# High parts behind the exponentials, modulation in the norm chains, and low parts shared by two engines

## The reference, cut to what matters

```python
h = rms_norm(x, norm_mix_pre[l])
proj = h @ w_in[l]                       # q, kv, gates of branch a, d, conformer, pooling
k_cmp = nsa_compress(k, ...)             # blocks of 32 keys -> 15 keys by a small MLP
o_a = g0 * o_cmp + g1 * o_slc + g2 * o_win   # three attentions over 8 heads
o_b = silu(layer_norm(causal_depthwise_conv(a * sigmoid(gate))))   # 31 taps
o_c = pool_mixer(c_in, pool_w[l], pool_scale[l])
o_d = banded_attention(..., SWA_WINDOW, swa_sinks[l])
up = einsum("bsnc,ncd->bsnd", [o_a, o_b, o_c, o_d], w_branch[l])
gates = sigmoid(h @ w_gate[l])           # 1024 x 4096
mix = sum_n(gates * up) @ w_o[l]
x = x + rms_norm(mix, norm_mix_post[l])
u = causal_depthwise_conv(rms_norm(x, ...) @ ffn_w_up[l], ffn_conv_w[l], ...)
x = x + rms_norm((gelu(gate) * val) @ ffn_w_down[l], norm_ffn_post[l])
```

## Time and profile before

| | |
|---|---|
| median of three runs | 2239.13 us |
| profiled execution, its span | 2239.11 us, 2237.3 us |
| TensorE matmul busy | 1869.7 us (84%) |
| VectorE, ScalarE, GpSimd busy | 1047.0, 754.9, 382.2 us |
| mean granted clock of TensorE | 0.879 |
| high parts in the first block (L404) | 118 of 1912 ns, ScalarE idle before them 404.2 us, of which 251.8 for a DMA |
| low parts by GpSimd (L410) | 26 of 4610 ns, 119.9 us |
| weight chunks | 256 of 1 MB, 4.8 us from issue to landing |

### The profile page before, as it was taken

The page is one execution under the profiler, slowest core; times in us unless marked ns, Lnnn a source line. Parts: engine busy times, 40 slices in busy tenths (PEclk is TensorE's granted clock), DMA queues, the critical chain, the costliest instruction groups (busy, mean ns, idle before and its releaser), DMA issues. The chain is left out here.

```text
span 2237.3 us, 26793 instructions
## 1 busy us (share of the span) xinstructions
PE 1869.7 (84%) x10780; PEld 1507.6 (67%) x10780; DVE 1047.0 (47%) x1452; ACT 754.9 (34%) x1055; POOL 382.2 (17%) x311
## 2 busy tenths in 40 slices
PE   7876767887988787676788799899989998899996
PEld 5765545877986566554587798654447653789996
DVE  4472324456653447232445665312844432545555
ACT  4332233444542333223344454211222330333341
POOL 0122220122540012222012244010142000100000
PEclk9987778898999898777889899979987999789998
DMA  5533122343545352313234354532211004235452
GB/s 216 201 110 132 76 113 94 114 151 123 188 159 198 108 206 106 132 76 112 94 115 150 125 186 166 191 138 72 79 38 38 1 1 150 76 133 188 179 179 92
DMA packets 39390, 279.99 MB, mean 125 GB/s; under 512 B 4464, under 2 KB 4720, under 8 KB 6384
## 3 DMA queue, kind: packets, MB, share of 16 engines
q1 hardware_dynamic: 37984, 272.44, 33.5%
q10 hardware_dynamic: 1296, 6.00, 0.7%
HBM read 277.37 MB, written 1.05 MB: 124 GB/s over the span
## 5 line engine op out<-in xcount | busy, mean ns | idle before, releaser
L404 ACT ACTIVATE sb_hi<-ring 128x2048 fp32r<-128x2048 f32 x118 | 225.7, 1912 | 404.2 <-DMA ring<-weights 251.8
L410 DVE TENSOR_TENSOR ring_low<-ring,sb_hi 128x2048 fp32r<-128x2048 f32 x92 | 211.7, 2303 | 231.6 <-ACT sb_hi L404 231.6
L545 PE MATMUL psum<-sb_hS,sb_hi 128*128 128x256 f32 x704 | 225.0, 320 | 40.3 <-DVE ring_low L410 25.2
L548 PE MATMUL psum<-sb_hS,sb_hi 128*128 128x256 f32 x704 | 218.6, 310 | 0.0
L549 PE MATMUL psum<-sb_hS,ring_low 128*128 128x256 f32 x704 | 216.9, 308 | 0.0
L777 PE MATMUL psum<-sb_hfT,ring_low 128*128 128x256 f32 x704 | 198.0, 281 | 0.0
L545 PEld LDWEIGHTS psum<-sb_hS,sb_hi 128*128 128x128 f32 x704 | 155.8, 221 | 55.5 <-DVE ring_low L410 32.1
L410 POOL TENSOR_TENSOR ring_low<-ring,sb_hi 128x2048 fp32r<-128x2048 f32 x26 | 119.9, 4610 | 426.0 <-ACT sb_hi L404 426.0
L1701 DVE TENSOR_TENSOR sb_split<-ring,sb_split 128x2048 fp32r<-128x2048 f32 x48 | 110.0, 2292 | 160.1 <-ACT sb_split L1696 160.1
L548 PEld LDWEIGHTS psum<-sb_hS,sb_hi 128*128 128x128 f32 x704 | 155.6, 221 | 0.0
L549 PEld LDWEIGHTS psum<-sb_hS,ring_low 128*128 128x128 f32 x704 | 155.5, 221 | 0.0
(11 more groups left out here) (382 smaller groups left out, 4392.1 us busy)
## 6 DMA issues: line engine op xcount, KB each, us to landing
ring<-weights SPq DMA_DIRECT2D x256, 1024.0 KB, 4.8
sb_rows<-rows ACTq DMA_DIRECT2D x1, 2048.0 KB, 9.8
sb_cols<-cols ACTq DMA_DIRECT2D x2, 694.0 KB, 6.2
sb_rows<-rows ACTq DMA_DIRECT2D x2, 516.0 KB, 6.9
sb_x<-x_in SPq DMA_DIRECT2D x1, 1024.0 KB, 5.1
sb_rows<-rows ACTq DMA_DIRECT2D x2, 512.0 KB, 3.7
sb_y<-ctx_in SPq DMA_DIRECT2D x1, 1024.0 KB, 5.6
out<-sb_x SPq DMA_DIRECT2D x2, 512.0 KB, 2.6
```

Of the source, the lines that this page charges most:

```text
L404: act.activation(hi_of(n), ring[:, c % SLOTS, :], ACT.Copy).then_inc(hi_ready, 1)
L410: eng.tensor_tensor(low_of(n), ring[:, SPLIT_CHUNKS[n] % SLOTS, :], hi_of(n).bitcast(F32), ALU.subtract)\
L545: mm = pe.matmul(out, hi[:, k, bs], hS[:, 0, k, :], start=(k == 0), stop=False)
L548: pe.matmul(out, hi[:, k, bs], hS[:, 1, k, :], start=False, stop=False)
```

## The change

It rearranges the first block's layers; the second block's program is not changed.

- **Attention.** In ScalarE's order the high part (`gate_hi`) stands behind the probability copies and the exponentials of the item. The modulation chunks are gone from this stretch. One padding chunk lies among the gates (behind the eighth) to keep the count at 92.
- **Low parts of gates 0 to 13** are made in two halves, columns 0 to 1023 by GpSimd and 1024 to 2047 by VectorE; TensorE waits for both.
- **Before attention.** The chunks of the compression MLP and those of ba and bg alternate (raw, ba, raw, ba, raw, bg, raw, bg). Pooling matmuls, compressed keys and compressed scores move behind gate 0 and gate 1, with their work on ScalarE and VectorE.
- **Modulation.** Three steps (six chunks) come after the output projection, three after the down projection of each layer. The rows are turned before and behind the transposes of the norm; the additions on VectorE follow in the norm chain.
- **FFN start.** The high and low parts of its first chunks are made later in the chain, the first low part ahead of the scaling of the turned rows.
- **Down projection** in the regions s0, s1, t and u.

```diff
-    out = ["split"] * 12 + ["raw"] * 4 + ["split"] * 2
-    for i in range(16):
-        out.append("split")
-        if mid_mod_of(i) is not None:
-            out.append("raw")
-    return out + ["split"] * (12 + FFN_CHUNKS) + ["raw"]
+    mods = ["raw"] * MOD_STEPS
+    gates = ["split"] * PAD_GATE + ["raw"] + ["split"] * (16 - PAD_GATE)
+    return ["split"] * FIRST_BA + ["raw", "split"] * 4 + gates + ["split"] * 12 + mods + ["split"] * FFN_CHUNKS + mods
...
+    for name in (("hid", 0), ("ba", 0), ("ba", 1), ("hid", 1), ("bg", 0)):
+        jobs.plan(name)
+    jobs.plan(("hidT", 0), "t", drains=2)
...
+    for i, r in zip(MODS_WO, "tus"):
+        jobs.plan(("mod", i), r)
+        jobs.plan(("modT", i), r)
...
-            jobs.plan(("down", c, t), f"a{2 * t + c}", drains=2)
+            jobs.plan(("down", c, t), ("s0", "s1", "t", "u")[2 * t + c], drains=2)
+    for kind in ("mod", "modT"):
+        for i in MODS_DOWN:
+            jobs.plan((kind, i))
...
     def split_lo(eng, n):
-        assert (n in POOL_LOWS) == (eng is nc.gpsimd)
+        half = slice(0, CH) if n not in POOL_LOWS else slice(CH // 2, CH) if eng is nc.vector else slice(0, CH // 2)
         eng.wait_ge(hi_ready, n + 1)
+        eng.tensor_tensor(low_of(n)[:, half], ring[:, SPLIT_CHUNKS[n] % SLOTS, half], hi_of(n)[:, half].bitcast(F32), ALU.subtract)\
+           .then_inc(lo_dve if eng is nc.vector else lo_pool, 1)
...  TensorE, attention
                 gate_chunks(1)
+                if i == 0:
+                    pool_mix()
+                    cmp_keys()
                 if i == 1:
+                    cmp_scores()
+                    gate_chunks(1)
                     cmp_out()
...  TensorE, behind the output projection
+            for i in MODS_WO:
+                mod_half(i, 0)
+                mod_half(i, 1)
+            for i in MODS_WO[:-1]:
+                mod_turn(i)
             for c in range(2):
                 for t in range(TT):
                     transpose4(("hf", c, t), ...)
+            mod_turn(MODS_WO[-1])
...  TensorE, behind the down projection
+            for i in MODS_DOWN:
+                mod_half(i, 0)
+                mod_half(i, 1)
+            for i in MODS_DOWN:
+                mod_turn(i)
...  ScalarE, attention
+            exps(0)
+            gate_out(1)
+            pool_out()
+            gate_hi()
+            for i in range(1, len(ITEMS) + 1):
                 if i >= 2:
                     out_copy(i - 2)
+                gate_out(1)
                 if i == 1:
+                    gate_hi()
+                    cmp_exps()
                     gate_out(1)
                     for t in range(TT):
                         copy_out(("cpT", t), ...)
+                turned_out(i - 1)
                 if i < len(ITEMS):
                     exps(i)
+                gate_hi()
...  VectorE, attention
+            mask(0)
+            split_lo(dve, FIRST_GATE + 1)
+            conv_steps(12)
+            pool_low()
+            cmp_blocks()
+            split_lo(dve, FIRST_GATE + 2)
+            for i in range(1, len(ITEMS) + 1):
                 if i < len(ITEMS):
                     mask(i)
+                weigh(i - 1)
...
                 conv_steps(10)
+                if i == 1:
+                    cmp_mask()
+                    cmp_weigh()
+                if FIRST_GATE + i + 3 in POOL_LOWS:
+                    split_lo(dve, FIRST_GATE + i + 3)
...  VectorE, norm chain behind the output projection
             residual("wo", 2)
-            split_lo(dve, FIRST_FFN + 1)
             dve.wait_ge(squares, 2 * TT)
             norm_tiles(3)
-            split_lo(dve, FIRST_FFN + 2)
+            mods_in(MODS_WO[:-1])
+            split_lo(dve, FIRST_FFN)
```

More of the change, by code:

```diff
@@ L261, in plan_layer @@
             jobs.plan(("O", a, t), "u", drains=2)
-    for i in range(16):
+    for i in range(2, 16):
         jobs.plan(("gate", i))
[L264 to L268, removed]
     for t in range(TT):
@@ L562, in _, with hid_half, hid_turn @@
                 transpose4(("rkT", t), [rot[:, t, i * P:(i + 1) * P] for i in range(3)])
[L563 to L580, removed]
+            def hid_half(kv, half):
+                chunk = next_chunk().rearrange("p (l h) -> p l h", l=8)
+                if half == 0:
+                    jobs.claim(pe, ("hid", kv))
+                    pe.wait_ge(flat_ready, 4 * kv + 5)
+                for lp in range(8):
+                    mm = pe.matmul(jobs.out(("hid", kv))[32 * (lp % 4):32 * (lp % 4) + 32, 0:T], flat32[:, kv, 8 * half + lp, :],
+                                   chunk[:, lp, :], start=(half == 0 and lp < 4), stop=(half == 1 and lp >= 4))
+                    if lp == 0:
+                        carry(mm)
+                if half == 1:
+                    jobs.fill(mm, ("hid", kv))
                 release(("hid", kv))
-            release(blocks_fm(("bg", 0)))
-            for kv in range(2):
+            def hid_turn(kv):
                 jobs.wait_drained(pe, ("hid", kv))
@@ L591, in _ @@
                 jobs.fill(mm, ("hidT", kv))
[L592 to L612, removed]
+            for kv in range(2):
+                for half in range(2):
+                    hid_half(kv, half)
+                    if (kv, half) == (1, 1):
+                        hid_turn(0)
+                        jobs.wait_drained(pe, "ga")
+                        jobs.claim(pe, "gaT")
+                        for t in range(TT):
+                            mm = pe.matmul(jobs.out("gaT")[:, 24 * t:24 * t + 24], gaT[:, t * P:(t + 1) * P], K("sel", 0, 24), start=True, stop=True)
+                        jobs.fill(mm, "gaT")
+                    release(blocks_fm((("ba", "bg")[kv], half)))
+            hid_turn(1)
             for t in range(TT):
@@ L617, in _ @@
                 transpose4(("rdT", t), [rot[:, t, 896 + i * P:896 + (i + 1) * P] for i in range(4)])
[L618 to L624, removed]
@@ L1320, in _ @@
                                   ALU.subtract).then_inc(mix_lo, 1)
-            for n in range(FIRST_WO + 1, FIRST_FFN + 1):
+            for n in range(FIRST_WO + 1, FIRST_FFN):
                 split_lo(dve, n)
@@ L2807, in rows_split @@
     return w.reshape(-1, 2, P, D).transpose(0, 2, 1, 3).reshape(-1, P, CH)
-def gates_and_mods(gate, mod):
-    out = []
-    for n in range(16):
-        at = 4 * BRANCH_ORDER[n // 4] + n % 4
-        out.append(gate[at:at + 1])
-        step = mid_mod_of(n)
-        if step is not None:
-            out.append(mod[step][n % 2:n % 2 + 1])
-    return out
 def layer_inputs(l, i):
@@ L2828, in layer_inputs @@
     br = {0: pairs(br[0], DH, 0), 1: br[1], 2: br[2], 3: pairs(br[3], DH, 0)}
+    cmp = i["nsa_cmp_w1"][l].reshape(2, 2, 8, P, 256).transpose(0, 1, 3, 2, 4).reshape(4, P, CH)
+    gate = n_split(i["w_gate"][l])
+    gate = [gate[4 * n + b] for n in BRANCH_ORDER for b in range(4)]
     chunks = [
```

265 lines of the change are left out of this document (143 added, 122 removed).

## The result

| | before | after |
|---|---|---|
| median of four runs each | 2239.67 us | 1984.27 us (1982.47 to 1987.12) |
| ratio, 95% interval | | 0.8861 (0.8846 to 0.8877) |
| profiled execution, its span | 2239.11, 2237.3 | 1983.36, 1981.6 |
| TensorE matmul busy (10780 matmuls in both) | 1869.7 | 1793.0 |
| span less that busy time | 367.6 | 188.6 |

The time fell by 255.4 us. Forecast was 2000.0 (1972 to 2070). The spans differ by 255.7: 179.0 is idle time of TensorE that went, and 76.7 is shorter matmuls. Their number is the same, so I read the second share as clock.

What follows compares the result with a forecast made beforehand. Attention was taken as bound by a chain: gate matmuls' end, transfer, high part, probability copy, value matmuls. Per layer -21 -52 -50 -7 +4 +6 = -120, two layers -240, from 2239 to 1999, rounded 2000 us (1972 to 2070).

Steps and rivals of the forecast that it cites:

- Part 1: Attention items: landing wait goes, small items 9.7 us, large 12.3; -52 and -50 us per layer.
- the two chains: Large items: TensorE's own work, 11.8 us, against a chain over all engines ending in VectorE's weighting, 11.8 or 12.4.
- Part 2: Low parts in halves: the engines exclude one another, VectorE first, 3.4 us; 0.65 per small item (absorbed), nothing in large.
- Part 3: Before the items: first ba block 7.7 us later, repaid by transfers no longer piling up; -21 us per layer.
- Part 4: Up to down projection: the 6.79 us idle before the down matmuls goes; -7 us per layer.
- The term of low clock: Down projection: about 1 us of low clock behind the stall there also goes.
- Part 5: Modulation in the norm chains: matmuls free, transfers not; FFN start +4, after the down projection +6 us per layer.
- The fourth rival: Faster: no slip in items (11.8 and 9.5), chains only +2 and +4; about 1985 us, within the forecast's own range.
- The first (the chain stays): Attention copies bound by something other than landing, only TensorE's moved modulation work goes; 2207 us, chance 0.06.
- The second (GpSimd first): GpSimd takes the lock first, each low part keeps VectorE 2.3 us longer; 2054 us, chance 0.18.
- the third: Slower: norm-chain modulation transfers one by one at 6.1 us, items still bound as before; 2333 us, chance 0.03.

Runs made afterwards that it cites:

- Run 3: The changed kernel with the low parts of gates 0 to 13 made whole on VectorE, none on GpSimd; 1996.92 us.
- run 4: The changed kernel with the low parts of gates 0 to 13 made whole on GpSimd, none on VectorE; 1999.31 us.
- run 6: The changed kernel with ScalarE's second ba high part behind the c and q copies, VectorE's low part behind its two copies, compressed mask and weights before the taps; 1955.96 us.
- Run 5: The changed kernel with the down projection back in the old banks a0 to a3; 2004.11 us.
- run 1: The changed kernel with ScalarE's high part put back ahead of the probability copies and exponentials in every attention item; 2063.02 us.

## Why the prediction came out, step by step

Times are of the first layer.

- **Part 1, items.** Small: 9.2 to 10.0 us from values to values (predicted 9.7). Large: 11.5 to 12.3 (12.3). Two sums of the prediction are not what their terms give: 1.16, 5.8, 0.66, 0.7 and 1.0 add to 9.3, not 9.5, and the terms of the large item to 11.7, not 11.8. The 2.3 us for a first item at the low clock did not come either: it took 9.5 us. From the third item to the first large one 48.1 us (51.6), from there to the end of the gates 81.3 (84): together -108 per layer in place of -102. The granted clock stayed at 1.00, for which the prediction had one pair of rows. In a large item VectorE's weighting ends at 240.84 and the transposes start at 240.89, so the two chains do tie; in the next two items TensorE waits 0.60 and 0.71 us for the weighting. Run 3 shows that a longer VectorE chain costs at once.
- **Part 2, halves.** The taps ahead of the third item, then VectorE and GpSimd in a small item:

```profile
145.27 6.20 DVE L1184 SCALAR_TENSOR_TENSOR sb_acc<-sb_bglu,sb_cols,sb_acc 128x256 f32<-128x256 f32 x10
...
161.28 1.22 DVE L395 TENSOR_TENSOR ring_low<-ring,sb_hi 128x1024 fp32r<-128x1024 f32 x1 [6.07 <-ACT sb_hi L388]
...
163.95 0.85 DVE L1259 TENSOR_TENSOR sb_small<-sb_small 128x4 f32<-128x4 f32 x1
164.83 0.69 DVE L1262 TENSOR_TENSOR sb_sc<-sb_sc,sb_small 128x512 f32<-128x512 f32 x1
```

```profile
161.39 3.39 POOL L395 TENSOR_TENSOR ring_low<-ring,sb_hi 128x1024 fp32r<-128x1024 f32 x1 [13.76 <-ACT sb_hi L388]
```

  VectorE goes first, as forecast, in 25 of the 28 low parts of the two layers. GpSimd's 3.39 us hold 1.11 of waiting (until 162.50) and 2.28 of work, the estimate being 2.26. The small product then waits until GpSimd is done at 164.78, 0.69 us longer than its 0.16; 0.65 was priced. Mask and maximum run beside GpSimd. The Trainium skill ("SBUF — State Buffer", section "Who interferes with whom") has this as a lock that the first to issue holds for its whole instruction; this trace and run 4 agree (2.67 us for a 128x4 product). Not priced was the place ahead of the third item: the ten taps at 145.27 stand behind the low part with GpSimd's half (144.24, 3.38 us) waiting, and took 6.20 us in place of 4.04. The compressed weights follow them, so by these rows some 2.2 of the 5.14 us wait for those weights come from the shared low part; no run tests that.
- **Part 3.** Transposes at 89.86 (predicted: with the copy at 90.5), first ba block 92.5 (92.8), first scores 124.4 (127.4), second item 134.0 (138.8), the wait for the compressed weights 5.14 us (about 5), third item 160.8 (163.5). Against before that is -24 instead of -21. The prediction read the new stall off the ring (which slot a chunk falls into), and run 6 shows that only an order of two instructions stood behind it: it could have been avoided. No run undoes the new order ahead of attention, so its -24 is read from the two traces alone.
- **Part 4.** The down projection follows the FFN without a gap and takes 61.5 us, 63.3 before: -8.6 where -7 was taken. Run 5 prices it at 20 us for both layers. The term of low clock was too small: without the stall the projection runs 1.8 us faster in the first layer here, and 2.8 in run 5.
- **Part 5.** FFN starts at +25.7 (predicted 24.7), +5 instead of +4. The next layer's transposes come at 29.7 behind the down projection, 19.4 before: +10.3 instead of +6. By its share this is the term that was mis-sized most. The last halves took 1.93 us and each turn 1.76, as TensorE was at the low clock, where the prediction had 1.07 and about 1.0; the last modulation sum came 18.9 us after the end, not 15.7. The end of layer 2, which has less behind it, moved by 6.2.
- **Sum.** Layer 1: -24 -56 -52 -8.6 +5 +10.3 = -125, and TensorE's first projection of layer 2 starts at 620.93 instead of 745.84. Layer 2 and the step into the second block bring 130: -24.1, -108.4 and -8.0 for the same places, and +4.9 and +6.2 for the chains. Predicted were 120 each. The 15 us between: parts 1, 3 and 4 brought 6 + 3 + 1.6 more per layer, 21 in all, and part 5 took 5.3 more in layer 1 and 1.2 in layer 2. So the forecast is near partly by luck, as these misses have opposite signs. The fourth rival (1985) is the nearest by its number, and that is luck too: its small items (9.5) and large ones (11.8) are about what came, but its chains (+2 and +4) cost +5 and +10.3, and it needed the larger gains of parts 3 and 4 to come out.
- **Rivals.** The first (the chain stays) fell by the trace. The second (GpSimd first) fell as well: it needs VectorE's low parts at 3.4 us, and they are at 1.22 in the items. Once per layer, behind the second item's scores (at 135.92 in the first), GpSimd did start first, and VectorE's low part took 2.08. Of the third, chunks came 6.1, then about 2.5 apart, as forecast.

## What to carry to other kernels

When an instruction waits for a DMA, look at what stands behind it in its engine's order before touching the transfers: moving a few lines gave 178 of 255 us by itself (79 on top of the rest of the change), and the late transfer stayed late. A queue in program order should have its waits sorted by who needs the result first, at the start of a stage too (run 6, 28 us more). Price a stall in a matmul stage twice, as idle time and as clock behind it: in run 1 the two were equal, in run 5 the clock was about a third of the idle time. Prefetched work put into idle chains is free only up to the depth of the ring.

## What the runs showed of the hardware

- One stall of 2.5 us in each item of 11 to 19 us brought the granted clock to 0.82 on average in the large items (run 1). Some items behind such a stall ran at the full clock and others at 1.2 GHz, where the scores took 3.78 us. A stall of 0.7 us, or two in a large item, left it at 1.00 in the changed kernel. The Trainium skill ("TensorE: Matmul & The Clock Gate", section "HAM oscillation — how this bites in real kernels") describes a loop of short bursts and waits for a DMA in which every wait takes the clock down. Run 1 agrees that waits which recur cost clock, with busy time up by 37.5 us at the same number of matmuls, but not that each one does, and its waits are shorter (2.5 us, against 3 to 5 in the page's loop) and are for a ScalarE copy.
- A recorded duration on VectorE or GpSimd holds the time for which the other has it locked out: 0.85 and 2.67 us for a product of 128x4 that takes 0.16, 3.39 for a half low part that takes 2.28.
- A wait of TensorE was put down to GpSimd (run 5) because its instruction ended 0.1 us ahead. The bank was freed by VectorE's, which ended 0.4 us ahead.
